# Input projections of a hybrid block: weight halves rounded and split into low parts in two steps of four blocks

## The chip, the cores and the metric

The kernel runs on one core of one Trainium2 chip. The metric is the device time of one execution in microseconds (us). The number of a kernel is the median of its runs.

## The reference

The reference is a two-layer block over 256 latent tokens and 256 context tokens of width 1024. The part that matters here is the mixer's input projection, once for each layer:

```
D_MODEL = 1024; D_INNER = 2048; SSD_WIDTH = 1024; CONF_WIDTH = SC_WIDTH = 512
SSD_IN = 1536 + 32;  IN_WIDTH = SSD_IN + SSD_WIDTH + 2 * CONF_WIDTH + 3 * SC_WIDTH   # 5152 columns

for i in range(DEPTH):                     # DEPTH = 2
    last = i == DEPTH - 1
    x, ctx = swiglu_half(x, ...), swiglu_half(ctx, ...)
    uc = modulate(ctx, norm_pre[i, 1], mc[3], mc[4])
    if last:
        xs, Bm, Cm, dt, A = ssd_inputs(uc @ w_in[i][:, :SSD_IN], ...)     # only the final states are needed
    else:
        yc, s_f, s_b = mixer(uc @ w_in[i], zero, zero, dwconv, dwconv, lp)
        ctx = swiglu_half(gated_residual(ctx, yc @ w_out[i], ...), ...)
    ux = modulate(x, norm_pre[i, 1], mx[3], mx[4])
    yx, _, _ = mixer(ux @ w_in[i], s_f, s_b, conv_along_rows, conv_along_cols, lp)
    x = swiglu_half(gated_residual(x, yx @ w_out[i], ...), ...)
```

`mixer` cuts the projection into x/B/C (through a five-tap convolution, then a chunked state-space scan in both directions), a gate z, a convolution of 31 taps with a layer norm, and a short gated convolution. All is fp32. The kernel keeps fp32 accuracy by splitting each matmul operand into a rounded high part and a low part, and adding three products: high weight by high input, high weight by low input, low weight by high input.

## The kernel before

Both streams lie side by side as 512 token columns. The input projection of one layer (`mix_in`) works through 40 halves, n = 0 to 39. A half is 128 output columns: eight 128 x 128 blocks of weights (k = 0 to 7), each used in three matmuls, 24 in all (L132, L133, L134 in `product_half`). In the first layer each matmul has 512 token columns. In the second layer the x/B/C halves 4 to 13 have 512 and all others 256, since context outputs are needed for the states alone. The list `HALVES` gives the order: gate and value (0 to 3), x/B/C (4 to 15), short convolution and the second gate and value (16 to 31), z (32 to 39).

For each half four engines work in a row, with two buffers (n % 2) for the split weights:

- SyncE loads a panel of two halves into `raw`, in one of two slots. It asks for panel p + 2 when both halves of panel p have their low parts.
- ScalarE rounds the half (`weight_hi`, L85): one instruction over 128 x 1024 elements, `wh` <- `raw`. It waits for the panel and for the product of half n - 2, whose buffer it overwrites, then raises `hi_done`. Behind it on ScalarE's queue, in the same turn of the loop, stand the readout of half n - 2 from PSUM and the other ScalarE work of the stage.
- GpSimd computes the low part (`weight_lo_pool`, L100): one subtraction over 128 x 1024, `wl` = `raw` - `wh`, after `hi_done`, and raises `lo_pool`. For halves 19 to 26, which run beside the first scan steps, VectorE does it instead (`weight_lo`, L93, signal `lo_done`). Halves 0 and 1 are split before the stage starts. That leaves 30 halves a layer to GpSimd, 60 in all.
- TensorE waits for the low part before the first matmul of the half (`plan.low_there`), and for the readout of the bank it fills.

The order on each engine is written out by hand in `mix_in`: after half 5 come the products for dt, after half 10 the cumulated sums, after half 12 a transpose; ScalarE has the exponentials and logarithms of dt before its halves 10 and 12, which VectorE feeds (L1505 to L1541); during halves 18 to 31 a generator lays the scan's matmuls between the blocks k (`after_k`), where VectorE multiplies the decay matrices (L1389, both inputs in SBUF); at halves 34 to 38 the layer-norm sums lie between the products. Behind the stage, `mix_out` multiplies by `w_out` in the same way with VectorE's low parts.

Of the kernel before, what the change touches and what calls it, by code (L numbers as in the profile page):

```python
# [15 lines left out]
ALU = mybir.AluOpType  # L16
ACT = mybir.ActivationFunctionType

P = 128
# [45 lines left out]
def r32(ap):  # L65

    return ap.bitcast(F32)
# [13 lines left out]
def weight_hi(K, act, panel_k, slot, half, kn, nth):  # L81

    act.wait_ge(K.raw_full[slot].sem, K.raw_full[slot].landed(panel_k))
    act.wait_ge(K.half_done.sem, K.half_done.at(nth - 1))
    ins = K.nc.scalar.activation(K.wh[:, half, 0:kn, :], K.raw[:, slot, 0:kn, half * P:half * P + P],  # L85
                                 ACT.Copy)
    ins.then_inc(K.hi_done.inc(), 1)
# [7 lines left out]
    ins.then_inc(K.lo_done.inc(), 1)  # L95


def weight_lo_pool(K, pool, slot, half, kn, nth):
    pool.wait_ge(K.hi_done.sem, K.hi_done.at(nth + 1))
    ins = K.nc.gpsimd.tensor_tensor(K.wl[:, half, 0:kn, :], K.raw[:, slot, 0:kn, half * P:half * P + P],  # L100
                                    r32(K.wh[:, half, 0:kn, :]), ALU.subtract)
    ins.then_inc(K.lo_pool.inc(), 1)


def split_ahead_act(K, act, halves=(0, 1)):
# [16 lines left out]
def product_half(K, pe, bank, half, kn, xh, xl, tok, first, last, nth, ready=None, after_k=None, low=None,  # L122
                 done="half"):


    t0, tn = tok
    pe.wait_ge(*(low or (K.lo_done.sem, K.lo_done.at(nth + 1))))
    for k in range(kn):
        if ready:
            pe.wait_ge(ready[0].sem, ready[0].at(ready[1] + k + 1))  # L130
        h, l = xh(k)[:, t0:t0 + tn], xl(k)[:, t0:t0 + tn]
        K.nc.tensor.matmul(bank[:, 0:tn], K.wh[:, half, k, :], h, start=first and k == 0, stop=False)  # L132
        K.nc.tensor.matmul(bank[:, 0:tn], K.wh[:, half, k, :], l, start=False, stop=False)  # L133
        ins = K.nc.tensor.matmul(bank[:, 0:tn], K.wl[:, half, k, :], h, start=False, stop=last and k == kn - 1)  # L134
        if after_k and k < kn - 1:
            after_k(k)
    if done:
        ins.then_inc((K.half_done if done == "half" else K.part_done).inc(), 1)
# [716 lines left out]
class ScanPlan:  # L855
# [9 lines left out]
    def low_there(self, K, n):  # L865
# [3 lines left out]
            return K.lo_done.sem, K.lo_done.at(len(on_dve))  # L869
        return K.lo_pool.sem, K.lo_pool.at(n + 1 - len(on_dve))  # L870

    def unit(self, n):

        seq = [s for s in self.seqs if self.with_y[s]][n // (8 * CHUNKS)]
        u = n % 8
        return u % 2, 2 * seq + n // 8 % CHUNKS, 4 * (u // 2)
# [42 lines left out]
SCAN_AT = XBC_AT + XBC_T + 2  # L919
# [4 lines left out]
Z_AT = HALVES.index(("z", 0))  # L924
# [31 lines left out]
def mix_in(K, M, layer, last, following):  # L956
# [8 lines left out]
    with ExitStack() as mem:  # L965
# [99 lines left out]
        def _(pe):  # L1065
# [94 lines left out]
            for n, (kind, tile) in enumerate(HALVES):  # L1160
                if n >= 2:
                    who = READER[HALVES[n - 2][0]]
                    read = K.act_read if who == "act" else K.dve_read
                    pe.wait_ge(read.sem, read.at(reads(n - 2, who)))
                if n == Z_AT:
                    for _ in scan:
                        pass
                if n == 0:
                    product_first_pair(K, pe, K.bank, uh, ul, part)
                elif n > 1:  # L1170
                    product_half(K, pe, K.bank[n % 2], n % 2, 8, lambda k: uh[:, k, :], lambda k: ul[:, k, :],
                                 FULL if kind == "xbc" and not alone(last, tile) else part, True, True, n, None,
                                 scan_step if SCAN_AT <= n < Z_AT else None, plan.low_there(K, n))
                if n == DT_AT - 1:

                    pe.wait_ge(K.dtw_ready.sem, K.dtw_ready.at(1))
                    for k in range(8):
                        for x, w in ((uh, wdh), (ul, wdh), (uh, wdl)):
                            ins = nc.tensor.matmul(K.bank[4][0:32, :], w[:, k, :], x[:, k, :],
                                                   start=k == 0 and w is wdh and x is uh, stop=k == 7 and w is wdl)  # L1180
                    ins.then_inc(K.dt_mm.inc(), 1)
                if n == DT_AT:
                    pe.wait_ge(K.dt_rows.sem, K.dt_rows.at(1))
                    for t in range(TT):
                        ins = nc.tensor.transpose(K.bank[4][:, 32 * t:32 * t + 32], dtr[:, t * P:t * P + P], K.ident[0:32, 0:32])
                    ins.then_inc(K.dt_raw.inc(), 1)
                if n == DT_AT + 4:

                    pe.wait_ge(K.dt_ready.sem, K.dt_ready.at(1))
                    for d in range(2):  # L1190
                        nc.tensor.matmul(K.bank[4][:, 64 * d:64 * d + 64], K.tri[:, d, :], a[:, :, d, :], start=True, stop=True)
                    ins = nc.tensor.matmul(K.bank[4][:, P:2 * P], K.ones[:, :], a[:, :, :, :].rearrange("p t d h -> p (t d h)"),
                                           start=True, stop=True)
                    ins.then_inc(K.cum_ready.inc(), 1)
                if n == DT_AT + 6:
                    pe.wait_ge(K.cum_read.sem, K.cum_read.at(1))
                    ins = nc.tensor.transpose(K.bank[4][:, 2 * P:3 * P], cum[:, :, :, :].rearrange("p d t h -> p (d t h)"), K.ident[:, :])
                    ins.then_inc(K.cumt_mm.inc(), 1)
                if n == LN_MEAN:

                    pe.wait_ge(K.conv_done.sem, K.conv_done.at(GRP_T))
                    for t in range(GRP_T):
                        ins = nc.tensor.matmul(K.bank[7][:, 0:pn], K.ones[:, :], conf[:, t, p0:p0 + pn], start=t == 0, stop=t == GRP_T - 1)
                    ins.then_inc(K.mean_ready.inc(), 1)
                if n in (LN_SQ, LN_SQ + 1):
                    for t in (0, 1) if n == LN_SQ else (2, 3):
                        pe.wait_ge(K.sq_ready.sem, K.sq_ready.at(t + 1))
                        sums_pe(K, pe, K.sq[:, t % 2, :], (0, pn), 0, t == 0, t == GRP_T - 1)
                if n == NH - 2:
                    rstd_pe(K, pe, pn, 1, 0)  # L1210

        @block.scalar
        def _(act):
# [35 lines left out]
            act.wait_ge(K.pads_zero.sem, K.pads_zero.at(4))  # L1249
            for n in range(NH + 2):  # L1250
                if 2 <= n < NH:
                    weight_hi(K, act, n // 4, n // 2 % 2, n % 2, 8, n)
                if n == 2:
                    act.wait_ge(K.dtw_in.sem, K.dtw_in.at(16))
                    nc.scalar.activation(wdh[:, :, :], wdt[:, :, :], ACT.Copy).then_inc(K.dtw_hi.inc(), 1)
# [698 lines left out]
def hybrid_block(nc, inputs, out):  # L1954
    K = Kern()
# [7 lines left out]
    with ExitStack() as ctx:  # L1963
# [5 lines left out]
        def signal(name):  # L1969

            K.signals.append(Signal(ctx.enter_context(nc.semaphore(name))))
            return K.signals[-1]
# [36 lines left out]
        K.half_done = signal("half_done")  # L2009
        K.hh_done = signal("hh_done")  # L2010
        K.hi_done = signal("hi_done")
        K.hl_done = signal("hl_done")
        K.ln_ready = signal("ln_ready")
        K.lo_pool = signal("lo_pool")
# [108 lines left out]
```

## Time and profile before

| | |
|---|---|
| runs of the kernel | 2281.19, 2286.88, 2287.19 us; median 2286.88 us |
| profiled execution, its own time | 2283.76 us |
| its span in the trace | 2282.0 us |
| TensorE matmul busy | 2138.3 us (94%), 12057 matmuls |
| VectorE / ScalarE / GpSimd busy | 1080.0 us / 840.3 us / 219.7 us |
| input projection and scan, first layer | about 476 to 805 us of the span |
| the same, second layer | about 1762 to 1995 us |

A row of the timeline gives the start and the length of an instruction in microseconds, the engine (PE is TensorE's matmul, PEld its weight load, DVE VectorE, ACT ScalarE, POOL GpSimd), the line of the kernel, the operation with the tensors it writes and reads, and in brackets how long the engine stood idle before it and who released it. Matmuls are pipelined: each row's length overlaps the next, so the distance between two starts is what a matmul costs. A row of busy time by stage gives the stretch, its length, then the busy time and the number of instructions of PE, PEld, DVE, ACT and POOL, the granted TensorE clock as a share of full speed, and the share and rate of the DMAs. A row by line gives the count, the shortest, median and longest duration in ns, and the first and last start.

### The profile page before, as it was taken

To read this page: it belongs to the slowest core of one execution; us is meant where nothing else is said; L and a number is where in the kernel's file an instruction comes from. 1 tells how busy PE (TensorE), PEld (TensorE's weight loads), DVE (VectorE), ACT (ScalarE), POOL (GpSimd) and SP (SyncE) were. 2 spreads that over 40 slices of the span, in tenths; PEclk is the share of its full clock that TensorE was granted. 3 is DMA by queue.
4 is the path that set the end of the run, shared out by engine and by line. 5 is a ranking of instruction groups with operands and counts; after the bars stand their busy time and mean duration, and the time that the engine had idled before them with its cause. 6 is when DMAs were issued, how large, how long until landed. Compare 5 with 4: busy or idle time off the path is not lost. (4 is left out here: it accounts for less than half of the span.)

```text
span 2282.0 us, 29070 instructions
## 1 busy us (share of the span) xinstructions
PE 2138.3 (94%) x12057; PEld 1750.1 (77%) x12057; DVE 1080.0 (47%) x1687; ACT 840.3 (37%) x1376; POOL 219.7 (10%) x160
## 2 busy tenths in 40 slices
PE   6999999998889989899999989999998988889998
PEld 4777777867556768677777778888787766788998
DVE  4232332459778652623322253333226678755554
ACT  3222222335355343422222233232224444554443
POOL 0000000133212300100000010000002342400000
PEclk9999999999999989899999989999998999999999
DMA  7545544222333212345544512222421233333553
GB/s 280 178 161 183 179 154 146 75 77 75 94 92 111 70 60 93 125 159 178 184 164 163 191 56 92 93 93 94 169 88 58 85 103 116 124 129 125 180 185 120
DMA packets 282834, 291.08 MB, mean 128 GB/s; under 512 B 8318, under 2 KB 275534, under 8 KB 282702
## 3 DMA queue, kind: packets, MB, share of 16 engines
q1 hardware_dynamic: 281671, 286.95, 38.5%
q8 instruction: 95, 1.56, 0.3%
q10 hardware_dynamic: 1031, 2.28, 0.3%
q14 instruction: 37, 0.30, 0.0%
HBM read 288.02 MB, written 1.18 MB: 127 GB/s over the span
## 5 line engine op out<-in xcount | busy, mean ns | idle before, releaser
L93 DVE TENSOR_TENSOR split<-raw,split 128x1024 fp32r<-128x1024 f32 (+1 forms) x308 | 369.7, 1200 | 876.2 <-ACT split L85 876.0
L85 ACT ACTIVATE split<-raw 128x1024 fp32r<-128x1024 f32 (+1 forms) x368 | 382.8, 1040 | 1090.1 <-PE bank L134 1073.6
L132 PE MATMUL bank<-uh,split 128*128 128x512 f32 (+1 forms) x1344 | 493.0, 367 | 1.1 <-DVE split L93 1.1
L133 PE MATMUL bank<-ul,split 128*128 128x512 f32 (+1 forms) x1344 | 488.6, 364 | 0.0
L134 PE MATMUL bank<-uh,split 128*128 128x512 f32 (+1 forms) x1344 | 487.4, 363 | 0.0
L132 PEld LDWEIGHTS bank<-uh,split 128*128 128x128 f32 x1344 | 253.6, 189 | 57.6 <-issue 18.4
L132 PE MATMUL bank<-hh,split 128*128 128x256 f32 (+1 forms) x836 | 283.0, 339 | 2.2 <-DVE split L93 2.2
L134 PEld LDWEIGHTS bank<-uh,split 128*128 128x128 f32 x1344 | 253.7, 189 | 40.4
L133 PEld LDWEIGHTS bank<-ul,split 128*128 128x128 f32 x1344 | 253.7, 189 | 38.0
L133 PE MATMUL bank<-hl,split 128*128 128x256 f32 (+1 forms) x836 | 279.1, 334 | 0.0
L134 PE MATMUL bank<-hh,split 128*128 128x256 f32 (+1 forms) x836 | 278.6, 333 | 0.0
L132 PE MATMUL bank<-mix_uh,split 128*128 128x512 f32 (+1 forms) x608 | 230.6, 379 | 28.4 <-POOL split L100 16.0
L134 PE MATMUL bank<-mix_uh,split 128*128 128x512 f32 (+1 forms) x608 | 215.9, 355 | 0.0
L133 PE MATMUL bank<-mix_ul,split 128*128 128x512 f32 (+1 forms) x608 | 215.7, 355 | 0.0
L132 PEld LDWEIGHTS bank<-hh,split 128*128 128x128 f32 x836 | 158.6, 190 | 27.4 <-issue 9.6
L134 PEld LDWEIGHTS bank<-hh,split 128*128 128x128 f32 x836 | 158.7, 190 | 16.1
L100 POOL TENSOR_TENSOR split<-raw,split 128x1024 fp32r<-128x1024 f32 x60 | 144.0, 2399 | 278.4 <-ACT split L85 278.4
L133 PEld LDWEIGHTS bank<-hl,split 128*128 128x128 f32 x836 | 158.7, 190 | 14.8
L386 POOL TENSOR_TENSOR res<-res,y 128x256 f32<-128x256 f32 x35 | 26.5, 774 | 1454.4 <-DVE y L371 1454.2
L132 PEld LDWEIGHTS bank<-mix_uh,split 128*128 128x128 f32 x608 | 116.8, 192 | 57.3 <-issue 26.6
L133 PEld LDWEIGHTS bank<-mix_ul,split 128*128 128x128 f32 x608 | 117.2, 193 | 16.4 <-issue 3.1
L134 PEld LDWEIGHTS bank<-mix_uh,split 128*128 128x128 f32 x608 | 116.8, 192 | 16.1
(225 smaller groups left out, 2485.1 us busy)
## 6 DMA issues: line engine op xcount, KB each, us to landing
raw_mod<-in_w_mod SPq DMA_DIRECT2D x64, 1024.0 KB, 7.4
raw<-in_ffn_w_gate SPq DMA_DIRECT2D x44, 1024.0 KB, 5.2
raw<-in_ffn_w_up SPq DMA_DIRECT2D x44, 1024.0 KB, 5.2
raw<-in_w_in SPq DMA_DIRECT2D x40, 1024.0 KB, 5.1
raw<-in_ffn_w_down SPq DMA_DIRECT2D x32, 1024.0 KB, 4.8
raw<-in_w_out SPq DMA_DIRECT2D x16, 1024.0 KB, 4.7
raw<-in_ffn_w_down SPq DMA_DIRECT2D x16, 768.0 KB, 4.5
decay<-cum_rows SPq DMA_DIRECT2D x48, 256.0 KB, 3.5
```

The source lines that it names most:

```text
L85: ins = K.nc.scalar.activation(K.wh[:, half, 0:kn, :], K.raw[:, slot, 0:kn, half * P:half * P + P], ACT.Copy)
L93: ins = K.nc.vector.tensor_tensor(K.wl[:, half, 0:kn, :], K.raw[:, slot, 0:kn, half * P:half * P + P], r32(K.wh[:, half, 0:kn, :]), ALU.su ...
L100: ins = K.nc.gpsimd.tensor_tensor(K.wl[:, half, 0:kn, :], K.raw[:, slot, 0:kn, half * P:half * P + P], r32(K.wh[:, half, 0:kn, :]), ALU.su ...
L132: K.nc.tensor.matmul(bank[:, 0:tn], K.wh[:, half, k, :], h, start=first and k == 0, stop=False)
L133: K.nc.tensor.matmul(bank[:, 0:tn], K.wh[:, half, k, :], l, start=False, stop=False)
L134: ins = K.nc.tensor.matmul(bank[:, 0:tn], K.wl[:, half, k, :], h, start=False, stop=last and k == kn - 1)
L386: ins = K.nc.gpsimd.tensor_tensor(K.res[:, j, t0:t0 + CTX], K.res[:, j, t0:t0 + CTX], y[:, j, a:a + CTX], ALU.add)
```

## The change

ScalarE rounds a half of the weights in two instructions of four blocks each (128 x 512 elements), and each raises a signal of its own (`hi_first`, `hi_done`). This holds for all halves 2 to 39. GpSimd takes the low parts of its 30 halves a layer in two subtractions, the first after `hi_first`, the second after `hi_done`, with signals `lo_first` and `lo_pool`. TensorE waits for the first signal before block 0 and for the second before block 4. VectorE's halves 19 to 26 keep one subtraction, after `hi_done`, and TensorE one wait. Loads wait for `lo_pool` as before, which now is the end of the second subtraction. Halves 0 and 1, and all other stages, are as they were.

```
+def weight_hi_parts(K, act, panel_k, slot, half, nth):
+
+    act.wait_ge(K.raw_full[slot].sem, K.raw_full[slot].landed(panel_k))
+    act.wait_ge(K.half_done.sem, K.half_done.at(nth - 1))
+    for done, k in ((K.hi_first, slice(0, 4)), (K.hi_done, slice(4, 8))):
+        ins = K.nc.scalar.activation(K.wh[:, half, k, :], K.raw[:, slot, k, half * P:half * P + P], ACT.Copy)
+        ins.then_inc(done.inc(), 1)
+
+
 def weight_lo_pool(K, pool, slot, half, kn, nth):
-    pool.wait_ge(K.hi_done.sem, K.hi_done.at(nth + 1))
-    ins = K.nc.gpsimd.tensor_tensor(K.wl[:, half, 0:kn, :], K.raw[:, slot, 0:kn, half * P:half * P + P],
-                                    r32(K.wh[:, half, 0:kn, :]), ALU.subtract)
-    ins.then_inc(K.lo_pool.inc(), 1)
+
+    for high, count, done, k in ((K.hi_first, nth - 1, K.lo_first, slice(0, 4)), (K.hi_done, nth + 1, K.lo_pool, slice(4, 8))):
+        pool.wait_ge(high.sem, high.at(count))
+        ins = K.nc.gpsimd.tensor_tensor(K.wl[:, half, k, :], K.raw[:, slot, k, half * P:half * P + P],
+                                        r32(K.wh[:, half, k, :]), ALU.subtract)
+        ins.then_inc(done.inc(), 1)
...
     t0, tn = tok
-    pe.wait_ge(*(low or (K.lo_done.sem, K.lo_done.at(nth + 1))))
+    low = low or ((K.lo_done.sem, K.lo_done.at(nth + 1)), None)
     for k in range(kn):
+        if k % 4 == 0 and k < 8 and low[k // 4]:
+            pe.wait_ge(*low[k // 4])
...
+    def low_parts(self, K, n):
+
+        if n < 2 or n in self.lo_on_dve:
+            return self.low_there(K, n), None
+        count = n + 1 - len([i for i in range(n + 1) if i < 2 or i in self.lo_on_dve])
+        return (K.lo_first.sem, K.lo_first.at(count)), (K.lo_pool.sem, K.lo_pool.at(count))
...
-                                 scan_step if SCAN_AT <= n < Z_AT else None, plan.low_there(K, n))
+                                 scan_step if SCAN_AT <= n < Z_AT else None, plan.low_parts(K, n))
...
-                    weight_hi(K, act, n // 4, n // 2 % 2, n % 2, 8, n)
+                    weight_hi_parts(K, act, n // 4, n // 2 % 2, n % 2, n)
```

On GpSimd, at the start of the first layer's projection, 17 subtractions stand in a row before the change (`L100`; then come the scan's products `xw`):

```order
L1041 MEMSET xbc_pad 128x1040
L100 TENSOR_TENSOR split<-raw,split 128x1024 [waits hi_done] x17
L1058 TENSOR_TENSOR xw<-xd,dec 128x512 [waits state_mm,xd_ready,decay_ready]
```

and after it the same place reads (the first two halves; the pair comes 17 times):

```order
L1060 MEMSET xbc_pad 128x1040
L111 TENSOR_TENSOR split<-raw,split 128x512 [waits hi_first]
L111 TENSOR_TENSOR split<-raw,split 128x512 [waits hi_done]
L111 TENSOR_TENSOR split<-raw,split 128x512 [waits hi_first]
L111 TENSOR_TENSOR split<-raw,split 128x512 [waits hi_done]
```

No instruction has moved past another there: each subtraction became two.

On TensorE, half 2 of the first layer (`mix_uh` and `mix_ul` are the high and low input; `act_read` is the readout of the bank) begins before the change with the one wait for the whole low part:

```order
L132 MATMUL bank<-mix_uh,split 128x512 [waits lo_pool,act_read]
L133 MATMUL bank<-mix_ul,split 128x512
L134 MATMUL bank<-mix_uh,split 128x512
L132 MATMUL bank<-mix_uh,split 128x512
L133 MATMUL bank<-mix_ul,split 128x512
```

and after it with the wait for the first part, and a second wait twelve matmuls on:

```order
L144 MATMUL bank<-mix_uh,split 128x512 [waits lo_first,act_read]
L145 MATMUL bank<-mix_ul,split 128x512
L146 MATMUL bank<-mix_uh,split 128x512
...
L144 MATMUL bank<-mix_uh,split 128x512 [waits lo_pool]
L145 MATMUL bank<-mix_ul,split 128x512
L146 MATMUL bank<-mix_uh,split 128x512
```

The matmuls and their order are the same; only what they wait for differs.

## Rows read from the trace of the kernel before

**Rows 1.** Part 5 of the page: the group of GpSimd's low parts.

```profile
L100 POOL TENSOR_TENSOR split<-raw,split 128x1024 fp32r<-128x1024 f32 x60 | 144.0, 2399 | 278.4 <-ACT split L85 278.4
```

**Rows 2.** Busy time by stage: halves 2 to 17, first and second layer.

```profile
476.00:584.00 108.00, 99.88 (x435) 79.28 (x434) 74.88 (x114) 51.17 (x73) 40.70 (x17) 0.98 0.29 89
1762.00:1854.00 92.00, 84.12 (x431) 69.83 (x431) 60.60 (x110) 49.09 (x72) 40.68 (x17) 0.96 0.29 88
```

**Rows 3.** Waits over the whole span: total, times, longest, in us.

```profile
PE bank L132 <- POOL split L100: 16.0, 10, 4.9
```

**Rows 4.** Timeline, second layer, end of half 13 to the start of half 16.

```profile
1840.10 0.39 PE L134 MATMUL bank<-mix_uh,split 128*128 128x512 f32 x1
1840.32 0.28 PE L132 MATMUL bank<-mix_uh,split 128*128 128x256 f32 x1
1840.58 1.06 ACT L85 ACTIVATE split<-raw 128x1024 fp32r<-128x1024 f32 x1 [2.66 <-PE bank L134]
1844.26 0.35 PE L132 MATMUL bank<-mix_uh,split 128*128 128x256 f32 x1 [0.90 <-POOL split L100]
1847.20 0.30 PE L132 MATMUL bank<-mix_uh,split 128*128 128x256 f32 x1
```

**Rows 5.** Timeline, second layer, halves 2 to 4.

```profile
1762.12 1.06 ACT L85 ACTIVATE split<-raw 128x1024 fp32r<-128x1024 f32 x1 [1.72 <-PE bank L156]
1765.08 1.05 ACT L85 ACTIVATE split<-raw 128x1024 fp32r<-128x1024 f32 x1
1765.75 0.36 PE L132 MATMUL bank<-mix_uh,split 128*128 128x256 f32 x1 [2.32 <-POOL split L100]
1767.64 0.42 PE L134 MATMUL bank<-mix_uh,split 128*128 128x256 f32 x1
1773.74 0.47 PE L132 MATMUL bank<-mix_uh,split 128*128 128x512 f32 x1 [0.53 <-DVE conf_pad L1477]
```

**Rows 6.** Timeline, first layer, before and at half 2.

```profile
476.30 1.06 ACT L85 ACTIVATE split<-raw 128x1024 fp32r<-128x1024 f32 x1 [2.36 <-PE bank L156]
478.50 0.39 PE L156 MATMUL bank<-mix_uh,split 128*128 128x512 f32 x1
479.96 0.47 PE L132 MATMUL bank<-mix_uh,split 128*128 128x512 f32 x1 [1.07 <-POOL split L100]
```

**Rows 7.** Timeline, first layer, half 12.

```profile
546.95 1.04 ACT L85 ACTIVATE split<-raw 128x1024 fp32r<-128x1024 f32 x1
550.61 0.47 PE L132 MATMUL bank<-mix_uh,split 128*128 128x512 f32 x1 [0.69 <-POOL split L100]
```

**Rows 8.** Timeline, second layer, halves 11 and 12.

```profile
1818.73 1.05 ACT L85 ACTIVATE split<-raw 128x1024 fp32r<-128x1024 f32 x1
1822.35 0.77 PE L132 MATMUL bank<-mix_uh,split 128*128 128x512 f32 x1 [2.60 <-POOL split L100]
1824.58 1.04 ACT L85 ACTIVATE split<-raw 128x1024 fp32r<-128x1024 f32 x1
1829.30 0.39 PE L132 MATMUL bank<-mix_uh,split 128*128 128x512 f32 x1
```

**Rows 9.** Instructions of smaller shapes, by line, and one from the timeline.

```profile
L1058 POOL TENSOR_TENSOR xw<-xd,dec x24: 1039/1046/2018, 592.7 to 1901.1; 128x512 f32<-128x512 f32 x24
L386 POOL TENSOR_TENSOR res<-res,mix_y x15: 722/728/920, 913.1 to 2063.8; 128x256 f32<-128x256 f32 x15
478.98 0.60 ACT L1264 ACTIVATE gate<-bank 128x512 f32<-128x512 f32 x1
```

**Rows 10.** Timeline, second layer: a VectorE product and the scan matmul behind it.

```profile
1919.45 2.39 DVE L1389 TENSOR_TENSOR decay<-decay,cb 128x512 f32<-128x512 f32 x1
1921.90 0.33 PE L1141 MATMUL bank<-decay,xd 128*64 128x128 f32 x2 [1.26 <-DVE decay L1389]
```

**Rows 11.** Timeline, second layer, half 38.

```profile
1984.27 1.04 ACT L85 ACTIVATE split<-raw 128x1024 fp32r<-128x1024 f32 x1
1987.92 0.36 PE L132 MATMUL bank<-mix_uh,split 128*128 128x256 f32 x1
```

More of the change, by code:

```diff
@@ L2011, in hybrid_block @@
         K.hi_done = signal("hi_done")
+        K.hi_first = signal("hi_first")
+        K.lo_first = signal("lo_first")
         K.hl_done = signal("hl_done")
```

## The prediction, made before the changed kernel ran

> **What bounds the kernel now.** I read the views in this order: busy time of the engines, busy time by stage, the waits, and then the timeline around the halves that wait. TensorE is busy for 94% of the span, so only places where it stands still can give time back. The change touches the two input projections alone. In halves 2 to 17 TensorE is busy for 99.9 of 108 us in the first layer and for 84.1 of 92 us in the second [rows 2]. The list of waits puts 16.0 us in 10 places on GpSimd's low parts [rows 3]. A wait for several signals is booked under one name only, so the timeline has to be read half by half: one more of them, half 4 of the second layer, stands there under a readout by VectorE [rows 5].
>
> The chain of a half is: the product of half n - 2 ends, ScalarE rounds (1.06 us), GpSimd subtracts (2.40 us on average [rows 1]), TensorE starts. Half 15 of the second layer shows it whole: ScalarE starts at 1840.58, TensorE at 1844.26, so 3.68 us, of which 0.22 are handovers [rows 4]. The product that should cover this is half 14. With 512 columns a half lasts 24 x 0.22 to 0.23 us, about 5.4, and covers it. With 256 columns it lasts 2.94 us (1844.26 to 1847.20) and doesn't: TensorE starts half 15 at 1844.26 and not at 1840.32 + 2.94 = 1843.26, one us lost in every second half [rows 4]. Where ScalarE or VectorE is late, at half 2 after the norm and at halves 10 to 12 behind dt, the whole 3.6 us stand open also with 512 columns [rows 6 to 8].
>
> **The new chain.** The smaller pieces are not in the trace. ScalarE: a copy of 512 elements from PSUM took 0.60 us [rows 9]; I take 0.62 us. GpSimd: a subtraction of 512 with its one operand repeated took 1.05 us, and 256 plain elements took 0.73 us [rows 9]; the line through 0.73 at 256 and 2.40 at 1024 gives 1.29 at 512. The bounds are 1.05 and 1.29; I take 1.27, since the operands are those of the 1024 form. The chain to the first matmul becomes 3.68 - (1.06 - 0.62) - (2.40 - 1.27) = 2.11 us, so it is 1.57 us shorter (1.55 to 1.79).
>
> The second part must be there when TensorE reaches block 4, twelve matmuls after the start: 1.47 us with 256 columns, 2.7 us with 512. It comes one GpSimd piece after the first, 1.27 us. That is enough, by 0.2 us where columns are 256. A wait already fulfilled costs TensorE nothing: over the seam of halves 13 and 14 the starts lie 0.22 us apart, like any others [rows 4].
>
> **Term by term** (gain at TensorE's start; after each of these places the rest of the stage follows TensorE, so the gain is carried).
> - First layer, half 2. The chain ends at 476.30 + 2.11 = 478.41. The product before it ends at 478.50 + 0.23 = 478.73, which now decides. 479.96 - 478.73 = 1.2 us [rows 6].
> - First layer, halves 10 to 12. ScalarE's starts there are set by VectorE's chain of dt and convolutions, which itself began with TensorE and so comes 1.2 us earlier. The gains of 10 and 11 are swallowed by it; only the last counts: 3.66 us from 546.95 to 550.61 become 2.11 [rows 7]. Another 1.55 us, 2.8 us for the layer. From half 13 on TensorE leads.
> - Second layer, halves 2 to 4. Half 2 starts at 1762.12 + 2.11 = 1764.23 instead of 1765.75. Before, it also ran into slow matmuls: one of 256 columns lasts 0.42 us at 1767.64 against 0.28 [rows 5, 4], and from its start to that of half 4 went 7.99 us, where two halves need 5.88. I assume that after a pause of 2.32 - 1.52 = 0.8 us its matmuls stay at the 2.4 GHz level; the granted clock of the first layer's stage, with a pause of 1.07 us at the same place, is 0.98 against 0.96 here [rows 2, 6]. Half 3 then starts at 1765.08 + 0.1 + 2.11 = 1767.3 and ends at 1770.2, and half 4 follows at once instead of at 1773.74: 3.5 us [rows 5]. The other end, if the clock falls all the same and half 4 is waited for as before, is the 1.5 us of the start alone.
> - Second layer, halves 11 and 12. The starts 1818.73 and 1824.58 of ScalarE are set by VectorE. Half 11 begins at 1820.84 and not 1822.35, and ends at 1826.3 if its matmuls are not slow; half 12 may begin at 1824.58 + 2.11 = 1826.7. Before: 1829.30 [rows 8]. 2.6 us; if half 11 is slow again (0.77 us for its first matmul before), 1.6 us.
> - Second layer, halves 15 and 17: twice 1.0 us [rows 4]. VectorE must keep pace there; it is busy for 61 of the stage's 92 us, which leaves room [rows 2].
> - Second layer, halves 34 to 38. For half 38, ScalarE starts at 1984.27 and TensorE at 1987.92 [rows 11]: 3.65 becomes 2.11, 1.5 us. What half 34 gives earlier is inside this, or small; I add nothing.
> - Scan. A decay product of VectorE over 512 elements lasted 2.39 us beside GpSimd's subtraction, and TensorE waited 1.26 us for it [rows 10]. After the first subtraction it can go, 1.1 us sooner (2.40 - 1.27) and a little more, since the first subtraction also starts earlier. I count 1.3 us for this place and nothing for the smaller ones. The Trainium skill (SBUF — State Buffer, Who interferes with whom) has this as a rule: a VectorE instruction with two SBUF inputs and a GpSimd one that reads SBUF exclude each other for a whole instruction. The trace agrees, 2.39 us. The rule also cuts the other way, and that is the third rival.
> - First-layer scan and z halves, 512 columns: TensorE leads or waits for VectorE; nothing.
>
> Sum of gains: 2.8 + 3.5 + 2.6 + 2.0 + 1.5 + 1.3 = 13.7 us.
>
> **What it costs.** Two ScalarE pieces instead of one: 2 x 0.62 against 1.06 is 0.18 us by the durations, but back to back they overlap, so I take 0.1 us (0 to 0.18). It stands in all 76 halves; under TensorE's product it is hidden. It shows where ScalarE is in the chain: some ten halves (10 to 12, and scan halves where VectorE waits for an exponential), 1.0 us. GpSimd holds 0.14 us more per half, hidden, since its end is earlier or later by 0.1 us only and a load is asked for two halves ahead. Loads keep their order on SyncE's queue and move with TensorE. The Trainium skill (VectorE: DVE Perf Modes, The TRN2 errata) speaks against this change: ScalarE pays a fixed 224 cycles per SBUF instruction. By its figures a half would cost 0.187 us more as an estimate, and ten of them 1.9 us instead of 1.0, which leaves the sum 0.9 us smaller.
>
> Net: 13.7 - 1.0 = 12.7 us. From the profiled execution, 2283.76 - 12.7 = 2271.1 us. That execution lies 3.1 us under the median of the runs; from the median it is 2286.88 - 12.7 = 2274.2 us. I predict the middle, 2272.5 us.
>
> **Rivals.**
> 1. The clock falls as before and the scan gives nothing back: 13.7 - 2.0 - 1.0 - 1.3 = 9.4, less 1.0 for ScalarE: 8.4 us, 2277 us. For it: these pauses shrink but don't vanish. Against it: the first layer's stage has such pauses of 1.07 and 0.69 us [rows 6, 7] and a clock of 0.98.
> 2. The gains stop at the stage where they arise. VectorE's work is fixed and fills 75 of 108 us and later more; if it, and not TensorE, carries the scan, then the 1.55 us pieces of halves 12 and 15 to 17 are waited off again and only the starts (1.2 + 3.5) and the end (1.5) stay: 6.2 - 1.0 = 5 us, 2280 us. Against it: before the scan VectorE has a third of the stage free [rows 2], and the scan starts when TensorE turns the x tiles.
> 3. Slower: the lock on both sides. Two subtractions mean two grabs of the port that VectorE needs. If VectorE, when refused, meets both parts and not one, each half holds it 0.14 us longer, and GpSimd's second part, refused in its turn by a product (I take 0.7 us, near ScalarE's 0.60 over as many elements [rows 9]), comes after TensorE has reached block 4. Price: with a second part 0.7 us late and 0.2 us of room, 0.5 us in each of the 30 halves of the second layer, 15 us, and 76 x 0.1 = 7.6 us on ScalarE if it is in every chain: 22.6 - 13.7 = 9 us slower, 2294 us. It decides from the point at which a second part takes over 1.47 us to arrive. Against it: most VectorE work beside the subtractions accumulates in PSUM and has one SBUF input.
> 4. The parts do not start apart: GpSimd's piece costs not 1.27 but nearly 2 us. Then the chain is 2.8 us, the gains halve, and block 4 waits with 256 columns: 2281 us.
>
> **How the numbers follow.** Forecast 0.5, first rival 0.22, second 0.16, third 0.04, fourth 0.08. A difference under 0.3% (6.9 us) can't be told from none in this kernel. Forecast and first rival are faster, the second is about half and half with the spread of the runs, the fourth mostly same: faster 0.79, same 0.17, slower 0.04. The range takes in 18 us of gain from the lower base (short pieces of 1.05 us, both clock terms, more of the scan's waits) and the second rival's 2280: 2265 to 2281 us.
>
> **What would show it.** GpSimd's pieces at 1.2 to 1.3 us, twice 60 of them; ScalarE start to first matmul of halves 15 and 17 at 2.1 us, or no wait at all, and halves 14 to 18 of the second layer 2.94 us apart; no slow matmuls in halves 2 and 11 there; the wait for GpSimd's low part nearly gone from the list; the first layer's half 13 about 2.8 us earlier and the second layer's stage about 11 us shorter. The prediction is wrong if TensorE waits at block 4, if half 18 of the second layer is not about 8 us earlier measured from the stage's begin, or if the scan there gets longer by what the halves before it gained.

## The result, and the profile after

| | before | after |
|---|---|---|
| median of the runs (5 each, one comparison) | 2287.16 us | 2274.63 us |
| range of the runs | 2281.19 to 2287.95 | 2270.20 to 2276.84 |
| ratio, 95% interval | | 0.9946 [0.9935, 0.9958] |
| profiled execution / its span | 2283.76 / 2282.0 us | 2274.84 / 2273.1 us |

The changed kernel is 12.5 us faster in this comparison; 12.7 us were forecast. In a second comparison, with 17 runs of the kernel before, it is 9.0 us faster (experiment 1), so the gain is known to some 3 us. The head of the profile page after the change (busy time by engine):

```profile
PE 2143.9 (94%) x12057; PEld 1754.6 (77%) x12057; DVE 1063.0 (47%) x1687; ACT 846.6 (37%) x1452; POOL 232.8 (10%) x220
```

Two numbers are new. VectorE has the same 1687 instructions and 17 us less busy time (1080.0 before). TensorE is busy for 5.6 us more (2138.3 before) with the same matmuls, so part of them ran at the lower clock. Both come back below.

The new pieces, by line (count, then shortest / median / longest in ns), and the waits of TensorE that matter (total, times, longest, in us):

```profile
L103 ACT ACTIVATE split<-raw x152: 612/620/635, 477.2 to 1977.5; 128x512 fp32r<-128x512 f32 x152
L111 POOL TENSOR_TENSOR split<-raw,split x120: 1262/1294/1819, 477.9 to 1978.9; 128x512 fp32r<-128x512 f32 x120
```
```profile
PE bank L1160 <- DVE decay L1408: 12.5, 11, 2.0
PE bank L144 <- ACT xbc_pad L1299: 6.6, 4, 3.6
PE bank L144 <- ACT gate L1283: 2.7, 2, 1.9
```

ScalarE's piece is the 0.62 us of the forecast, GpSimd's 1.29 instead of 1.27. The 16.0 us that TensorE stood for GpSimd's low parts [rows 3] are gone from the list. In their place stand two readouts by ScalarE (`xbc_pad`, `gate`), and the wait for VectorE's decay products is shorter: it was 16.3 us in 13 places.

**Where the time came from.** I took the start of the first matmul of each half, measured from the first matmul of the projection in that layer (463.73 and 1750.36 us before, 464.62 and 1747.76 us after). The gain at a half is the difference to before; "end" is the first matmul of the output projection behind the stage. From one column of the table to the next one sees what the halves between gave.

| half | 2 | 4 | 9 | 12 | 18 | 22 | 27 | 30 | 32 | 39 | end |
|---|---|---|---|---|---|---|---|---|---|---|---|
| first layer, after | 0.2 | 0.2 | 0.2 | 1.8 | 1.7 | 3.4 | 3.3 | 4.1 | 4.7 | 4.7 | 4.7 |
| first layer, second profile of the same kernel | 0.6 | 0.6 | 0.6 | 2.1 | 2.0 | 2.2 | 0.8 | 1.7 | 2.2 | 2.2 | 2.2 |
| second layer, after | 0.5 | 2.7 | 2.8 | 4.0 | 6.3 | 3.3 | 4.9 | 5.2 | 6.6 | 8.1 | 7.7 |
| second layer, second profile | 0.6 | 2.7 | 2.8 | 4.1 | 6.3 | 3.4 | 4.9 | 5.2 | 6.8 | 8.3 | 7.9 |

The two stages together give 4.7 + 7.7 = 12.4 us. The two spans differ by 8.9 us only: in this execution the stages that the change doesn't touch took 3.5 us more than in the profiled execution of before. The medians differ by 12.5.

**Half 2.** The timeline after the change, first layer and second layer:

```profile
478.24 0.40 ACT L1274 ACTIVATE wdh<-wdt 128x256 fp32r<-128x256 f32 x1
478.66 1.28 ACT L1283 ACT_TABLE_LOAD   x1
479.96 0.60 ACT L1283 ACTIVATE gate<-bank 128x512 f32<-128x512 f32 x1
480.61 0.50 PE L144 MATMUL bank<-mix_uh,split 128*128 128x512 f32 x1 [0.83 <-ACT gate L1283]
```
```profile
1760.89 1.28 ACT L1283 ACT_TABLE_LOAD   x1
1762.18 0.38 ACT L1283 ACTIVATE gate<-bank 128x256 f32<-128x256 f32 x1
1762.62 0.39 PE L144 MATMUL bank<-mix_uh,split 128*128 128x256 f32 x1 [1.90 <-ACT gate L1283]
```

TensorE also waits for the readout of the bank it fills, and that readout stands behind the rounding, a copy and a load of ScalarE's function table. The low part was ready earlier; the readout is late next. Of 1.2 and 1.5 us only 0.2 and 0.5 were left.

**Halves 14 to 18, second layer** (the answer to [rows 4]):

```profile
1833.94 0.63 ACT L103 ACTIVATE split<-raw 128x512 fp32r<-128x512 f32 x1 [2.57 <-PE bank L146]
1834.65 1.29 POOL L111 TENSOR_TENSOR split<-raw,split 128x512 fp32r<-128x512 f32 x1 [2.82 <-ACT split L103]
1835.89 1.31 POOL L111 TENSOR_TENSOR split<-raw,split 128x512 fp32r<-128x512 f32 x1
1836.55 0.28 PE L144 MATMUL bank<-mix_uh,split 128*128 128x256 f32 x1
1839.43 0.28 PE L144 MATMUL bank<-mix_uh,split 128*128 128x256 f32 x1
```

These are half 15's pieces, and the starts of halves 15 and 16. The first piece ends at 1835.94, 0.6 us before TensorE wants it; there is no pause. The halves start 2.88 us apart.

**Half 11, second layer** (the answer to [rows 8]):

```profile
1814.84 0.59 ACT L1299 ACTIVATE xbc_pad<-bank 128x512 f32<-128x512 f32 x1
1815.48 0.50 PE L144 MATMUL bank<-mix_uh,split 128*128 128x512 f32 x1 [1.99 <-ACT xbc_pad L1299]
1816.54 0.63 PE L144 MATMUL bank<-mix_uh,split 128*128 128x512 f32 x1
1817.82 0.63 PE L144 MATMUL bank<-mix_uh,split 128*128 128x512 f32 x1
```

Again a readout ends the wait, and after it three matmuls take 1817.82 - 1816.54 = 1.28 us, 0.43 each, where 0.23 is normal: the lower clock. The granted clock of 1815 to 1820 us reads 0.66 (0.67 in the same place before).

**The scan.** One product of VectorE with both inputs in SBUF, and the subtraction beside it, before and after:

```profile
787.57 2.39 POOL L100 TENSOR_TENSOR split<-raw,split 128x1024 fp32r<-128x1024 f32 x1 [5.24 <-ACT split L85]
788.00 2.50 DVE L1569 TENSOR_TENSOR xbc<-xbc,gate 128x512 f32<-128x512 f32 x1 [5.13 <-ACT gate L1269]
```
```profile
783.34 1.29 POOL L111 TENSOR_TENSOR split<-raw,split 128x512 fp32r<-128x512 f32 x1 [4.65 <-ACT split L103]
784.30 0.88 DVE L1588 TENSOR_TENSOR xbc<-xbc,gate 128x512 f32<-128x512 f32 x1 [6.76 <-ACT gate L1288]
784.59 1.74 POOL L111 TENSOR_TENSOR split<-raw,split 128x512 fp32r<-128x512 f32 x1
```

Before, the product ends 0.54 us after the whole subtraction. After, it ends 0.55 us after the first piece, and the second piece takes 1.74 us and not 1.29: VectorE got in between the two. This product shows the port and no gain: it stands in the first layer's z halves, where TensorE's gain stays at 4.7 us from half 32 to half 39. The group by line, of before and of after (busy us, mean ns):

```profile
L1569 DVE TENSOR_TENSOR xbc<-xbc,gate 128x512 f32<-128x512 f32 x8 | 11.0, 1388 | 18.7 <-ACT gate L1269 18.7
```
```profile
L1588 DVE TENSOR_TENSOR xbc<-xbc,gate 128x512 f32<-128x512 f32 x8 | 6.0, 756 | 22.8 <-ACT gate L1288 22.8
L1408 DVE TENSOR_TENSOR decay<-decay,cb 128x512 f32<-128x512 f32 x48 | 38.2, 797 | 17.0 <-ACT decay L1261 17.0
```

The products of 256 elements in the second layer's z halves go from 1388 to 727 ns. The decay products, 844 ns in the mean before, lose 2.2 us in all. The product of [rows 10], 2.39 us long, now takes 0.75.

**Halves 20 to 22, second layer: 3.0 us lost.** The timeline before, then after:

```profile
1871.21 0.38 PE L132 MATMUL bank<-mix_uh,split 128*128 128x256 f32 x1 [2.63 <-DVE sc_pad_x L1482]
1871.67 1.88 PE L1093 MATMUL bank<-xw,b_tm 128*128 128x512 f32 x4
1881.40 0.39 PE L132 MATMUL bank<-mix_uh,split 128*128 128x256 f32 x1 [2.62 <-DVE sc_pad_x L1482]
1881.85 1.88 PE L1093 MATMUL bank<-xw,b_tm 128*128 128x512 f32 x4
```
```profile
1862.64 0.39 PE L144 MATMUL bank<-mix_uh,split 128*128 128x256 f32 x1 [2.63 <-DVE sc_pad_x L1501]
1873.88 0.49 PE L144 MATMUL bank<-mix_uh,split 128*128 128x256 f32 x1 [2.62 <-DVE sc_pad_x L1501]
1874.59 3.29 PE L1112 MATMUL bank<-xw,b_tm 128*128 128x512 f32 x4
```

The pauses are the same 2.6 us. After them four state matmuls take 3.29 us instead of 1.88. The busy time in these stretches (length, PE busy, granted clock, DMA) of before, then of after:

```profile
1871.00:1876.00 5.00, 4.05 (x16) 1.00 0.00 0
1881.00:1887.00 6.00, 4.86 (x29) 1.00 0.59 175
```
```profile
1863.00:1868.00 5.00, 4.83 (x14) 0.66 0.00 0
1874.00:1880.00 6.00, 5.26 (x19) 0.72 0.60 175
```

So the granted clock fell from the 2.4 GHz level towards the 1.2 GHz one, behind pauses behind which it had not fallen before.

**Half 31, second layer: a fall that went away.** TensorE behind its wait for the last decay product, before and after:

```profile
1957.68 0.66 PE L1141 MATMUL bank<-decay,xd 128*64 128x128 f32 x8 [2.16 <-DVE decay L1389]
1958.27 1.96 PE L1116 MATMUL bank<-ident,y_tm 128*128 128x128 f32 x8
```
```profile
1949.88 0.66 PE L1160 MATMUL bank<-decay,xd 128*64 128x128 f32 x8 [2.03 <-DVE decay L1408]
1950.46 1.16 PE L1135 MATMUL bank<-ident,y_tm 128*128 128x128 f32 x8
```

These eight matmuls and eight more behind them take 3.45 us before and 1.89 us after; the granted clock is 0.60 from 1957.6 to 1961.8 us before and 1.00 from 1949.8 to 1954 us after. So 1.5 of the 3.4 us that halves 23 to 32 give here are matmuls that were slow before. The direct part is shorter waits, above all the 1.26 us of [rows 10].

### The profile page after: what moved, and what is told of

Read it like the earlier page. It is cut to its first block and busy times, and to the rows that moved or that the text cites. A ratio compares the mean times of both kernels' runs of the same rounds, so it can differ in the third digit from the quotient of the medians.

```text
span 2273.1 us, 29206 instructions
## 1 busy us (share of the span) xinstructions
PE 2143.9 (94%) x12057; PEld 1754.6 (77%) x12057; DVE 1063.0 (47%) x1687; ACT 846.6 (37%) x1452; POOL 232.8 (10%) x220
## 5 line engine op out<-in xcount | busy, mean ns | idle before, releaser
L85 ACT ACTIVATE split<-raw 128x1024 fp32r<-128x1024 f32 (+1 forms) x292 | 302.3, 1035 | 894.0 <-PE bank L146 879.8
L111 POOL TENSOR_TENSOR split<-raw,split 128x512 fp32r<-128x512 f32 x120 | 157.4, 1333 | 251.8 <-ACT split L103 251.8
L144 PEld LDWEIGHTS bank<-mix_uh,split 128*128 128x128 f32 x608 | 116.9, 192 | 48.8 <-issue 12.6
L103 ACT ACTIVATE split<-raw 128x512 fp32r<-128x512 f32 x152 | 87.3, 622 | 179.0 <-PE bank L146 174.7
```

Of the source, the lines that this page charges most:

```text
L103: ins = K.nc.scalar.activation(K.wh[:, half, k, :], K.raw[:, slot, k, half * P:half * P + P], ACT.Copy)
L111: ins = K.nc.gpsimd.tensor_tensor(K.wl[:, half, k, :], K.raw[:, slot, k, half * P:half * P + P], r32(K.wh[:, half, k, :]), ALU.subtract)
```

## The experiments

My theory after the result: three things pay. TensorE starts a half earlier; VectorE gets the port back after half a subtraction; and some slow matmuls go. ScalarE's split pays for nothing. The main rival: the early start of TensorE is all that pays, and the rest is noise of the clock. The kernels ran in two groups, each beside the kernel before: 2285.13 us (17 runs) in the first group, 2285.86 us (12 runs) in the second. Gains by half are in the sense of the table above.

**1. The changed kernel once more.** Nothing edited.

> The changed kernel unchanged, timed again beside the others and with a second profile. Theory: the time is 2270 to 2277 us again, and the gains at halves 10 to 18 and in the z halves stand at the same places to 0.1 us, since the handovers between engines set them. The slow matmuls at halves 20 and 21 of the second layer, which took 3.0 us back in the first profile, hang on how the 2.9 us pauses there fall: I expect them in some executions only, so about 1 chance in 2 here. Rival: they come with the change (the shorter pauses before them), then they stand at the same place again with 3 us.

Measured: 2276.10 us, ratio 0.9956 [0.9944, 0.9968], which is 9.0 us under the kernel before in its group. The second layer is the same within 0.2 us, the loss at halves 20 to 22 included. The first layer gains 2.2 us, not 4.7. The matmuls of half 25 were slow here, 1.6 us. The other 1.2 us arise in half 21, where the clock falls in both profiles: here, as before the change, behind a wait for a decay product, in the first profile ahead of it, so that the slow matmuls were hidden in the wait. Apart from that the layers agree: from half 27 to half 32 the first layer gains 1.4 us in both profiles.

**2. ScalarE in two pieces alone.** GpSimd keeps one subtraction, TensorE one wait.

```
 def weight_lo_pool(K, pool, slot, half, kn, nth):
+    pool.wait_ge(K.hi_done.sem, K.hi_done.at(nth + 1))
+    ins = K.nc.gpsimd.tensor_tensor(K.wl[:, half, 0:kn, :], ...)      # one subtraction, as before
...
+        return self.low_there(K, n), None
```

> ScalarE rounds in two pieces, but GpSimd subtracts the whole half after the second, and TensorE waits once for all of it. Theory: only the cost of the ScalarE part is left, 0.1 us later for each low part and each instruction behind it, on some 10 to 15 halves of the chain: 1 to 2 us slower than before, 2288 to 2289 us. Rival (a fixed cost of a ScalarE instruction falls on every half in the chain, 0.19 us on 30 or more halves): 5 us or more slower, 2292 us.

Measured: 2287.91 us (11 runs), ratio 1.0008 [0.9999, 1.0018]; by half it is 0.6 us late at the end of the first stage and 0.9 us at the end of the second. The cost of the pieces is 1.5 us in the profile, with slow matmuls gone at half 11 of the second layer (1.0 us) and come at half 22 (0.9 us), and nothing that can be told from zero in the median. A pair takes 1.14 to 1.15 us where the whole took 1.06 [rows 4], so 0.09 us a half.

**3. GpSimd in two pieces alone.** ScalarE rounds in one instruction, both subtractions wait for it.

```
-    for high, count, ... in ((K.hi_first, nth - 1, K.lo_first, slice(0, 4)), (K.hi_done, nth + 1, K.lo_pool, slice(4, 8))):
+    for high, count, ... in ((K.hi_done, nth + 1, K.lo_first, slice(0, 4)), (K.hi_done, nth + 1, K.lo_pool, slice(4, 8))):
...
-                    weight_hi_parts(K, act, n // 4, n // 2 % 2, n % 2, n)
+                    weight_hi(K, act, n // 4, n // 2 % 2, n % 2, 8, n)
```

> ScalarE rounds a half whole as before; GpSimd subtracts in two parts, TensorE waits in two. Theory: the chain is 3.68 - 2.40 + 1.29 = 2.57 us, which still hides behind a 256-column half of 2.94 us, and the readout by ScalarE that now sets halves 2 and 11 is 0.1 us earlier: nearly the whole gain, 10 to 12 us, 2275 to 2277 us. Rival (each part of the chain carries its share): the 0.4 us of ScalarE missing at some 8 places cost 3 us or more of the 12.5, 2278 us or more.

Measured: 2273.19 us, ratio 0.9945 [0.9932, 0.9958]: not distinguishable from the whole change. Stages 3.7 and 7.1 us. Splitting the rounding isn't needed for this gain; splitting the subtraction is the change. One product in this kernel shows what the port takes:

```profile
784.29 2.98 POOL L111 TENSOR_TENSOR split<-raw,split 128x512 fp32r<-128x512 f32 x2 [4.65 <-ACT split L85]
784.73 1.40 DVE L1588 TENSOR_TENSOR xbc<-xbc,gate 128x512 f32<-128x512 f32 x1 [6.24 <-ACT gate L1288]
```

VectorE is released 0.44 us after GpSimd starts and takes 1.40 us; in the changed kernel 0.96 us after and 0.88 us; in the kernel before 0.43 us after a start of 2.39 us and 2.50 us. All three are what GpSimd's running piece has left, plus 0.55 us: 1.29 - 0.44 + 0.55 = 1.40, 1.29 - 0.96 + 0.55 = 0.88, 2.39 - 0.43 + 0.55 = 2.51. In the trace of before, 11 of the `xbc` and `decay` products of 512 elements start inside a subtraction, and all end 0.55 us behind it; the 5 of 256 elements end 0.28 us behind it. That it is the second SBUF input and not GpSimd's work as such, VectorE's convolution taps show, which have one input tensor in SBUF and the other in PSUM: 36 of those on `xbc_pad` start inside a subtraction there and take 756 ns, as the 52 others do.

**4. Both split, but TensorE waits for the whole low part.**

```
     def low_parts(self, K, n):
+        return self.low_there(K, n), None
```

> Everything in two parts as in the changed kernel, but TensorE waits before block 0 for the end of the second part. The chain to TensorE is then 0.62 + 2 x 1.29 + 0.3 = 3.5 us, only 0.2 us shorter than before. Theory: the gains at halves 2 to 18 and in z nearly vanish, while in the scan those of the shorter hold of the port stay (halves 22, 28, 30, 32 of the first layer and 27, 32 of the second, where a decay product of VectorE no longer waits 2.4 us): about 5 us faster than before, 2282 us. Rival (the scan's gains come from TensorE's earlier starts too): under 2 us, 2286 us.

Measured: 2275.71 us (6 runs, 2272.55 to 2280.78; the profiled one is the slowest), ratio 0.9957 [0.9945, 0.9970]. This was a miss: the kernel is as fast as the changed one. By half, the loss is there: half 18 of the second layer gains 3.7 us and not 6.3. But halves 20 to 22 lose nothing here (3.8 us at half 22, against 3.3), and half 23 only 0.9; from there to half 32 the stage wins 2.7 us without any early start, where the changed kernel wins 3.4 (1.5 us of either is half 31's clock), and it ends at 6.0 us. The first stage ends at 0.8 us. The two stages of this profile, the slowest run of six, thus explain 6.8 us of the 9.4 between the medians. The early start is worth 2.6 us up to half 18 of the second layer and 1.1 us in the first, and in the changed kernel the fall of the clock takes 3.0 us off.

**5. One subtraction from the scan on.** Halves up to 18 as changed, GpSimd's later halves in one subtraction.

```
+    if nth > SCAN_AT:
+        parts = ((K.hi_done, nth + 1, K.lo_pool, slice(0, 8)),)
...
-        if n < 2 or n in self.lo_on_dve:
+        if n < 2 or n > SCAN_AT:
```

> The changed kernel, but from half 27 on GpSimd subtracts a half whole and TensorE waits once, as before the change; halves 2 to 18 stay in two parts. Theory (the later gains come from the port: VectorE's products with two SBUF inputs get in between two subtractions): the gains of the scan at halves 27 to 32 (about 1.4 us in the first layer, 3.4 us in the second) and those of the z halves of the second layer (1.0 to 1.5 us) vanish, the mean of the VectorE products in the z halves is back at 1.39 us, and the time is 5 to 6 us above the changed kernel, about 2280 us. Rival (they come from earlier starts upstream): the scan's gains stay, and only 1 to 1.5 us of the z halves are lost, 2276 us.

Measured: 2280.95 us (8 runs), ratio 0.9975 [0.9963, 0.9987]: 4.9 to 6.3 us slower than the two comparisons of the changed kernel. The same product, the group and TensorE's wait are those of before again:

```profile
787.02 2.39 POOL L114 TENSOR_TENSOR split<-raw,split 128x1024 fp32r<-128x1024 f32 x1 [5.24 <-ACT split L103]
787.46 2.50 DVE L1591 TENSOR_TENSOR xbc<-xbc,gate 128x512 f32<-128x512 f32 x1 [5.13 <-ACT gate L1291]
```
```profile
L1591 DVE TENSOR_TENSOR xbc<-xbc,gate 128x512 f32<-128x512 f32 x8 | 11.1, 1399 | 18.7 <-ACT gate L1291 18.7
```
```profile
PE bank L1163 <- DVE decay L1411: 17.0, 13, 2.6
```

The second stage gains 6.6 us up to half 18, 6.3 in the changed kernel, and from half 22 on nothing more (3.5, 3.4, 3.3, 3.0 us at halves 22, 27, 32 and 39, where the changed kernel goes from 3.3 to 8.1). So what the split gives from the scan on, 4.7 us in this stage, comes from the late subtractions. In the first layer halves 27 to 32 give -0.3 us here, and 1.3 to 1.4 us in all seven profiles with the late subtractions in two: that gain is firm too, and it is shorter waits for VectorE. Experiment 4 has the late subtractions in two pieces, but no early start, and keeps 2.7 of 3.4 us up to half 32 and 0.7 of 1.5 us at halves 33 to 39 of the second layer: most of it needs no early start of TensorE. But it is not all VectorE's time either. The fall of the clock at half 31 is there in the three profiles with the late subtractions whole (before, experiments 2 and 5) and in none of the seven others, so 1.5 us of it come by way of the clock. The waits ahead of it last 2.2 to 2.5 us in the three and 1.8 to 2.7 us in the seven, so their length alone does not decide.

**6. The readout between the two roundings.** For halves up to 18, ScalarE does its first piece, then the readout of half n - 2, then the second piece, and the copy for dt last.

```
...                  # weight_hi_parts takes the list of pieces to do
-                    weight_hi_parts(K, act, n // 4, n // 2 % 2, n % 2, n)
...                  # the copy for dt at half 2 goes from here
+                    weight_hi_parts(K, act, n // 4, n // 2 % 2, n % 2, n, (0,) if n <= SCAN_AT else (0, 1))
...                  # the readout of half n - 2
+                if 2 <= n <= SCAN_AT:
+                    weight_hi_parts(K, act, n // 4, n // 2 % 2, n % 2, n, (1,))
+                if n == 2:
+                    act.wait_ge(K.dtw_in.sem, K.dtw_in.at(16))
+                    nc.scalar.activation(wdh[:, :, :], wdt[:, :, :], ACT.Copy).then_inc(K.dtw_hi.inc(), 1)
```

> In halves 2 to 18 ScalarE reads out half n - 2 between the two roundings, and at half 2 the small rounding for dt comes after them. Theory: halves 2, 11 and 12 now wait for this readout and not for the low part; it comes 0.9 to 1.0 us earlier at half 2 and 0.3 us at halves 10 to 12. First layer 1.0 + 0.3, second layer 1.0 + 0.3, so 2 to 2.6 us under the changed kernel, 2272 us. Rival (the second low part comes too late for block 4 in the 256-column halves, since its rounding stands behind the readout): 0.3 us lost in each of halves 14 to 18 of the second layer, which leaves 1 us or nothing.

Measured: 2269.52 us, ratio 0.9926 [0.9913, 0.9940]. Half 2 of the second layer:

```profile
1757.15 1.28 ACT L1280 ACT_TABLE_LOAD   x1
1758.45 0.38 ACT L1280 ACTIVATE gate<-bank 128x256 f32<-128x256 f32 x1
1758.73 0.62 ACT L103 ACTIVATE split<-raw 128x512 fp32r<-128x512 f32 x1
1758.89 0.39 PE L144 MATMUL bank<-mix_uh,split 128*128 128x256 f32 x1 [1.07 <-ACT gate L1280]
```

The gain at half 2 is 1.4 us in both layers, against 0.2 and 0.5: the readout was what stood in the way. The stage ends at 11.4 us, though, and the larger part of the difference (3.0 us of 3.7) is not there but at halves 20 to 22, where nothing is lost. The pauses there are as long as ever (the first of the two):

```profile
1858.91 0.39 PE L144 MATMUL bank<-mix_uh,split 128*128 128x256 f32 x1 [2.63 <-DVE sc_pad_x L1503]
1859.37 1.88 PE L1112 MATMUL bank<-xw,b_tm 128*128 128x512 f32 x4
```

**7. Matmuls in the pauses.** The changed kernel, with five matmuls of 256 columns on constants, into a bank that nobody reads, before the waits of halves 20 and 21 in the second layer.

```
+                    if last and n in (SCAN_AT + 2, SCAN_AT + 3):
+                        warm_pe(K, 5, 6)
```

> The changed kernel with five matmuls that nobody reads (256 fp32 columns each, into an idle bank, 0.4 us each) before the readout waits of halves 20 and 21 of the second layer, where TensorE stands still for 2.9 us. Theory: the 3.0 us that the scan of the second layer takes back there are slow matmuls after these pauses; with TensorE at work in them its matmuls stay at the 2.4 GHz level, and 2.5 to 3 us come back, 2272 us. Rival (the three us come from VectorE, whose work started earlier and waits for the same things): no change, or 0.3 us longer, 2275 us.

Measured: 2271.28 us, ratio 0.9934 [0.9922, 0.9947]. The pause is filled, and the matmuls behind it are quick:

```profile
1861.45 2.32 PE L416 MATMUL bank<-tri,ident 128*128 128x256 f32 x10
1864.24 0.38 PE L144 MATMUL bank<-mix_uh,split 128*128 128x256 f32 x1 [0.47 <-DVE sc_pad_x L1503]
1864.70 1.88 PE L1112 MATMUL bank<-xw,b_tm 128*128 128x512 f32 x4
```

(The five stand as ten in the trace.) The gain is 6.5 us at half 20 and still 6.5 at half 22, and 10.4 at the end of the stage. The first stage of this profile gains 1.0 us only, since there half 11 was slow (0.43 us a matmul). This shows that the 3.0 us were the clock, and that with TensorE at work in the pauses it does not fall.

**8. Edits 6 and 7 together.**

> Both of the edits of the two runs before together. If each gives what its theory says they add, 5 us under the changed kernel, 2269.5 us. Rival for the sum: the earlier starts move the pauses, so that the clock falls at another place, and only one of the two gains is seen, 2272 us.

Measured: 2268.28 us, ratio 0.9920 [0.9907, 0.9934], the fastest kernel here: 17.6 us under the kernel before in its group. The step from 2269.52 us is inside the spread of five runs (2265.93 to 2269.80 against 2267.95 to 2272.52): where edit 6 already avoids the fall, the extra matmuls have nothing left to save.

## Why the prediction was right, and where it was not

The sign and the size were right, 12.5 us for 12.7; that they agree to 0.2 us is luck, since the second comparison has 9.0 us. The forecast time, 2272.5 us, was 2.1 us too low, as it took the middle of two bases, 2271.1 and 2274.2 us. The chain that was forecast is what the traces show, but the terms were less right, and errors on both sides cancelled.

| term | forecast | profile after |
|---|---|---|
| first layer, half 2 | 1.2 | 0.2 |
| first layer, halves 10 to 12 | 1.55 | 1.5 |
| first layer, scan and z | 0 | 3.0 (0.2 in the second profile) |
| second layer, halves 2 to 4 | 3.5 | 2.7 |
| second layer, halves 11 and 12 | 2.6 (1.6 if slow) | 1.3, slow |
| second layer, halves 15 and 17 | 2.0 | 2.2 |
| second layer, halves 20 to 22 | none | -3.0 |
| second layer, halves 23 to 32 | 1.3 | 3.4 |
| second layer, halves 33 to 39 | 1.5 | 1.5 |
| ScalarE's pieces | -1.0 | -1.5 (experiment 2) |

The column of the profile after already holds the cost of ScalarE's pieces in its rows, so the last row isn't added to it; behind half 39 the second stage gives 0.5 us back, and 0.1 us came at half 5. With that the rows sum to 12.4 us.

- **The chain of a half.** Right: 0.62 and 1.29 us, the two parts apart, no pause in halves 14 to 18, and half 18 is 6.3 us early against the 8 forecast. What is missing is missing at halves 2 to 4 and 11. In the first layer the sum of halves 10 to 12 was right and the place was not: 1.3 us came at half 10, whose gain I had called swallowed, and under 0.1 us at half 12. The same holds for the second layer's z halves: 0.7 of the 1.5 us came at half 34, for which I had added nothing.
- **Half 2.** Here the step "the product before it ends at 478.73, which now decides" failed. The wait names one releaser, and I did not ask what else TensorE's first matmul waits for. The readout stood in ScalarE's queue right behind the rounding, with a table load before it, and decided. Experiment 6 gave 1.1 and 0.9 us of it back (half 2 at 1.4 in both layers, from 0.25 and 0.5).
- **Half 11.** The same: a readout ends the wait. The slow matmuls that I had taken as the smaller case came too.
- **The port.** The step that was mis-sized is "I count 1.3 us for this place and nothing for the smaller ones". What the split gives from the scan on in the second layer was 4.7 us by experiment 5, of which 1.5 had been counted as TensorE's; with the first layer it is 4.9 to 6.3 us by the medians. The place itself, half 26 of the second layer, gave 1.6 us in the first profile, near the 1.3. What I had put at nothing is 1.4 us of shorter waits in halves 27 to 32 of the first layer, some 0.3 us in the second, and the 1.5 us of the clock at its half 31. The Trainium skill (SBUF — State Buffer, Who interferes with whom) says that the two engines exclude each other for a whole instruction. The products of experiment 3 agree, to 0.01 us. What it means for a split is that the lock is held half as long at a time.
- **The third rival**, the lock grabbed twice, had its first half right: the second piece does take 1.74 us when a product gets in. It cost nothing that shows: three such products lie in the first layer's z halves, where the gain stays at 4.7 us.
- **The first rival's clock** was partly true: the slow matmuls stayed at half 11 and new ones came at halves 20 to 22. I had weighed the clock only where it had been slow before, not where a change of timing can make it slow.
- **ScalarE.** 0.09 us a half instead of 0.1. The Trainium skill (VectorE: DVE Perf Modes, The TRN2 errata) has a fixed cost per ScalarE instruction, 0.187 us a half as my estimate from it. Taken singly the pieces agree, 2 x 0.62 - 1.06 = 0.18 us; back to back half of it overlaps, 1.15 - 1.06 = 0.09. The sum over the stages, 1.5 us, lies between the 1.0 forecast and the 1.9 of the estimate; the slow matmuls that came and went in that profile make it no better than that.

The forecast thus missed 3.0 us lost to the clock and some 3 us at halves 2 to 4 and 11, and in the other direction 3.0 us in the first layer's scan and 2.1 in the second's. Of these 5.1 us some 2.9 are the clock once more (half 21 of the first layer, half 31 of the second). That it all cancels is luck.

## What stays open

Why the clock falls behind the pauses of halves 20 to 22 in one kernel and not in another is not settled. The pauses last 2.6 us in all of them. In one profile of each, the fall came in the changed kernel, its repeat and experiments 3 and 5, and not in the kernel before and experiments 2, 4 and 6 (in 2 and 4 it came at half 22, for 0.9 us); that looks as if it follows the kernel's timing rather than chance, but what in the timing, no run here separates. At half 11 of the second layer experiment 5 kept the full clock, though its instructions up to there are those of the changed kernel, which fell in both of its profiles. Why half 31's fall goes with the whole subtractions is open in the same way. The first layer's scan gains 0.2 to 3.0 us, of which the 1.4 us of halves 27 to 32 are firm and the rest is where the clock falls. A kernel with edit 6's order of the readout and GpSimd's split alone was not tried.

## What to carry to other kernels

When a wait is to be shortened, list everything the waiting instruction waits for, and put the next-latest beside the new chain: here it was a readout queued behind the very step that was made faster. Two engines that share a port are helped by shorter instructions on the one that nobody waits for, and that can be worth more than the pipelining for which it was split. A change that takes some us out of a stage moves the pauses behind it; check there whether the matmuls got slower or quicker before you book the gain to anything else. Idle matmuls in the pauses brought the loss back here.

## What the runs showed of the hardware that I had not expected

- A VectorE product with two SBUF inputs that has to wait for GpSimd is shown as a longer product, not as a wait: its length is the rest of GpSimd's instruction plus 0.55 us for 512 elements and 0.28 us for 256, and it goes in between two subtractions that stand back to back in GpSimd's queue, although the second is ready to go.
- A pause of TensorE of 2.6 us sometimes costs nothing and sometimes 1.4 us at the next four matmuls (3.29 against 1.88 us), and the same in both profiles of the changed kernel. Five matmuls of constants in it were enough here.
- Two ScalarE instructions of 0.62 us back to back take 1.14 us.
